# A hybrid encoder layer on one core: GLA between half-depth projection units, out-projection in two halves inside the attention stages, six places for experts

## What is computed

```python
z = rms_norm(x) @ w_in                      # 1024 -> 3088, cut into aq ak av gq gk gv ga gr
# group A, 4 heads: k and q normed; two softmax maps; chunk mask in the prompt, a cache of 512 keys per stream
p = softmax(q1 k1) - lam * softmax(q2 k2);  ao = rms_norm(p @ v) * (1 - lam_init)
# group B, 4 heads, GLA in chunks of 64 (prompt) or 16 (streams, with a state)
la = log_sigmoid(ga @ w_a2 + b_a) / 16;  b = cumsum(la)
o = (q k^T decayed by b) v + (q * exp(b)) S;  S = exp(b_last) * S + (k * exp(b_last - b))^T v
go = rms_norm(o) * silu(gr)
x = x + concat(ao, go) @ w_out
# top-1 of 4 groups, then top-2 of its 8 experts; 32 SwiGLU experts of width 256
x = x + sum_e combine_e * (silu(h @ w_gate[e]) * (h @ w_up[e])) @ w_down[e],  h = rms_norm(x)
```

## Time and profile before

| | |
|---|---|
| median of three runs | 748.46 us (747.38 to 749.25) |
| span of the profiled execution | 745.4 us; the runs lie 2.0 to 3.9 us above this span |
| granted TensorE clock, mean | 0.888 |
| busy: PE, PEld, DVE, ACT, POOL | 598.8, 395.4, 264.3, 186.4, 58.9 us |
| moved by DMA | 163.54 MB, 219 GB/s in the mean |
| chain that ended last | PE 60%, DMA 22%, DVE 8%, ACT 4%, issue 3% |

### The profile page before, as it was taken

How to read it: one execution, slowest core, us unless ns; L and a number is a source line. 1 busy time by engine, 2 the same in 40 slices (tenths; PEclk the granted TensorE clock), 3 DMA queues, 4 the chain that set the end, 5 groups by cost and what they waited for, 6 DMA issues and landing times.

```text
span 745.4 us, 8671 instructions
## 1 busy us (share of the span) xinstructions
PE 598.8 (80%) x3380; PEld 395.4 (53%) x3380; DVE 264.3 (35%) x542; ACT 186.4 (25%) x394; POOL 58.9 (8%) x93
## 2 busy tenths in 40 slices
PE   2699999999978978779799953998868687866940
PEld 2587888888865865548688843333223132322310
DVE  4811131336569447756753253110101010000006
ACT  4521233213271146556621020011010111101010
POOL 4000000000220010000000011021010102101010
PEclk9799999999996768879999955999989899989885
DMA  7011122131230176048651094499999999999639
GB/s 276 0 57 57 57 94 75 57 113 56 81 117 2 64 306 258 1 172 323 242 198 57 29 404 170 146 395 431 424 427 424 424 427 420 424 406 406 288 110 360
DMA packets 23507, 163.54 MB, mean 219 GB/s; under 512 B 4737, under 2 KB 5138, under 8 KB 10290
## 3 DMA queue, kind: packets, MB, share of 16 engines
q1 hardware_dynamic: 16290, 143.56, 48.1%
q0 software_dynamic: 6464, 16.92, 5.9%
q10 hardware_dynamic: 720, 2.62, 0.9%
HBM read 152.47 MB, written 17.43 MB: 228 GB/s over the span
## 4 chain that ended last, share of the span: by engine, by line
PE 60%; DMA 22%; DVE 8%; ACT 4%; issue 3%; POOL 1%; SPq 1%; ACTq 0%; POOLq 0%; DVEq 0%
DMA Zpad<-in_w_gu 19%; PE bank L1838 11%; PE bank L1448 7%; PE bank L1449 7%; PE bank L1450 7%; PE bank L1755 3%; PE bank L1757 3%; PE bank L1756 2%; DMA Zpad<-ye_dram 2%; PE bank L1860 2%; DVE mx L1150 1%; PE bank L1592 1%; PE bank L1776 1%; PE bank L1681 1%; PE bank L1603 1%
## 5 line engine op out<-in xcount | busy, mean ns | idle before, releaser
L1838 PE MATMUL bank<-Zpad,W 128*64 128x512 f32 x256 | 127.0, 654 | 13.6 <-DMA G<-in_w_gu 11.1
L1448 PE MATMUL bank<-W_r,hbuf_r 128*128 128x512 f32 x240 | 94.4, 393 | 3.4 <-issue 3.4
L1449 PE MATMUL bank<-W_r,hbuf_r 128*128 128x512 f32 x240 | 93.9, 391 | 0.0
L1450 PE MATMUL bank<-W_r,G_r 128*128 128x512 f32 x240 | 93.8, 391 | 0.0
L1838 PE MATMUL bank<-R,W 128*64 128x512 f32 x112 | 60.2, 699 | 30.4 <-DMA Zpad<-in_w_gu 29.5
L1394 DVE TENSOR_TENSOR W<-W,bank 128x256 f32<-128x256 f32 x16 | 6.8, 422 | 196.2 <-ACT W L886 196.2
L957 DVE TENSOR_TENSOR W_r<-W,W_r 128x2048 fp32r<-128x2048 f32 x12 | 27.5, 2291 | 104.7 <-ACT W_r L667 104.7
L1838 PEld LDWEIGHTS bank<-Zpad,W 128*64 128x64 f32 x256 | 37.1, 150 | 48.7 <-issue 45.8
L1860 PE MATMUL bank<-Zpad,W 128*64 128x512 f32 x128 | 57.9, 595 | 3.8 <-ACT W L890 3.8
L1838 PE MATMUL bank<-G,W 128*64 128x512 f32 x128 | 59.9, 623 | 0.0
L1838 PEld LDWEIGHTS bank<-R,W 128*64 128x64 f32 x112 | 17.3, 161 | 71.7 <-issue 71.7
(11 more groups left out here) (305 smaller groups left out, 983.8 us busy)
## 6 DMA issues: line engine op xcount, KB each, us to landing
Zpad<-in_w_gu SPq DMA_DIRECT2D x16, 2048.0 KB, 20.1
Zpad<-in_w_dn SPq DMA_DIRECT2D x16, 1024.0 KB, 25.8
G<-in_w_gu SPq DMA_DIRECT2D x8, 2048.0 KB, 24.2
R<-in_w_gu SPq DMA_DIRECT2D x7, 2048.0 KB, 19.0
W<-in_w_main SPq DMA_DIRECT2D x12, 1024.0 KB, 5.1
G<-in_w_dn SPq DMA_DIRECT2D x9, 1024.0 KB, 25.9
R<-in_w_dn SPq DMA_DIRECT2D x7, 1024.0 KB, 24.4
W<-in_cache_kt SPq DMA_DIRECT2D x4, 1024.0 KB, 5.6
```

The costliest lines, as they stand in the source:

```text
L1448: pe.matmul(bank[i][:, :], hH[:, d, i, :], wH[k][:, cols], start=(d == 0), stop=False)
L1449: pe.matmul(bank[i][:, :], hH[:, d, i, :], wL[k][:, cols], start=False, stop=False)
L1450: ins = pe.matmul(bank[i][:, :], hL[:, d, i, :], wH[k][:, cols], start=False, stop=(d == DC - 1))
L1838: ins = pe.matmul(bank[2 + q][CAP * j:CAP * j + CAP, :], xsT[q][:, c, j * CAP:(j + 1) * CAP], wgu[j][:, c, :], start=(c == 0), stop=(c == ...
```

## The change

It rewrites the memory plan as one arena of 49 K words per partition, and with it:

- x is transposed as loaded; norm1's gain goes into the weight halves and the token's scale into the evacuation. Weight halves are made in four slices.
- `proj(c, k, i)` is a unit of 12 matmuls. From chunk 2 on, 40 units are counted by `u`, and the pieces of GLA and the transposes of keys and queries stand between them at the units of the `U_` tables. Squares for the key and query norms, the key norm itself and the scaling of the attention outputs are GpSimd's.
- The out-projection has a GLA half (`g_step`, one step per round of the prompt attention from round 4) and an attention half (`a_step`, from round 4 of the stream attention; steps 7 to 14 behind it). A step is four transposes of a tile or twelve matmuls for half of its columns; both use one bank, 7, for tiles 0 and 1, and the sums are added to x twice.
- Keys and values of streams have three places, experts six, which are used in turn, pair by pair. The expert loops are written out.

```diff
+U_CUM, U_GT = 4, 6
+U_KT = (8, 10, 12)
+U_SC = (13, 15, 18, 20, 23)
+U_OUT = (15, 18, 20, 23, 29)
+U_SU = (25, 26, 27, 28)
+U_KTR, U_QTR = 31, 35
...
+        NKV = 3
+        EPLACE = [28 * KW, 34 * KW, 40 * KW, 5 * KW, 11 * KW, 17 * KW]
...
-            for b in range(NKV, NB):
-                sp.wait_ge(d_s_done, b - NKV + 1)
-                sp.dma_start(Kc[b % NKV], cache_kt[b]).then_inc(ld_k[b % NKV], 16)
-            for b in range(NKV, NB):
-                sp.wait_ge(d_pv_done, b - NKV + 1)
-                sp.dma_start(Vc[b % NKV], cache_v[b]).then_inc(ld_v[b % NKV], 16)
-            for n, c in enumerate(WO_ORDER):
-                sp.wait_ge(d_s_done if n < 2 else d_pv_done, NKV + n % 2 + 1)
-                sp.dma_start(wo[:, c:c + 2, :], w_out[:, c:c + 2, :]).then_inc(ld_x[n], 16)
-            sp.dma_start(egu[1], gu_rows(1)).then_inc(ld_gu[1], 16)
-            sp.dma_start(edn[1], dn_rows(1)).then_inc(ld_dn[1], 16)
-            sp.wait_ge(mT_done, 2 * NT)
-            sp.wait_ge(st_kv, 2 * NT * 16)
-            for e in (2, 0, 3):
-                if e == 0:
-                    sp.wait_ge(out_done, 2 * NT)
-                sp.dma_start(egu[e], gu_rows(e)).then_inc(ld_gu[e], 16)
-                sp.dma_start(edn[e], dn_rows(e)).then_inc(ld_dn[e], 16)
-            sp.dma_start(gu4, gu_rows(4)).then_inc(ld_gu[0], 16)
-            experts(0, 1, k0=1)
-            with sp.Fori(2, NE // 4) as g:
-                experts(0, g)
...
+                if c == 3:
+                    sp.wait_ge(b_done, 1)
+                    sp.dma_start(S0, state).then_inc(ld_state, 16)
+            sp.wait_ge(proj_done, NT * 6)
+            wo_half(H, 0)
+            wo_half(H, 1)
+            for i in range(NT):
+                sp.dma_start(X[:, i, :], x[i]).then_inc(ld_x[i], 16)
+            sp.wait_ge(st_states, 2 * 16)
+            for b in range(NKV):
+                sp.dma_start(Kc[b], cache_kt[b]).then_inc(ld_k[b], 16)
+                sp.dma_start(Vc[b], cache_v[b]).then_inc(ld_v[b], 16)
+            sp.wait_ge(out_done, 2 * NT)
+            wo_half(0, 0)
+            wo_half(0, 1)
+            for b in range(NKV, NB):
+                sp.wait_ge(d_s_done, b - NKV + 1)
+                sp.dma_start(Kc[b % NKV], cache_kt[b]).then_inc(ld_k[b % NKV], 16)
+                sp.wait_ge(d_pv_done, b - NKV + 1)
+                sp.dma_start(Vc[b % NKV], cache_v[b]).then_inc(ld_v[b % NKV], 16)
+            sp.wait_ge(d_s_done, NB)
+            sp.wait_ge(d_pv_done, NB)
+            sp.wait_ge(st_v, NT * 16)
+            for e in range(3):
+                gate_up_of(e)
+                down_of(e)
+            sp.wait_ge(out_done, 4 * NT)
+            for e in (3, 4):
+                gate_up_of(e)
+                down_of(e)
+            sp.wait_ge(tab_done, 1)
+            sp.wait_ge(idx_ready, 1)
+            gate_up_of(5)
+            down_of(5)
+            for e in range(NBUF, NE, 2):
+                sp.wait_ge(gu_done, e // 2 - 2)
+                gate_up_of(e)
+                gate_up_of(e + 1)
+                sp.wait_ge(dn_done, e // 2 - 2)
+                down_of(e)
+                down_of(e + 1)
...
+            def squares(c, kq):
+                for i in range(NT):
+                    pool.wait_ge(z_free, NT * c + i + 1)
+                    if kq:
+                        pool.wait_ge(kqred, i + 1)
+                    pool.tensor_tensor(z(C_V, i), z(c, i), z(c, i), ALU.mult).then_inc(kq_sq, 1)
+            squares(C_K, 0)
+            pool.wait_ge(rkq_ready, 1)
+            for i in range(NT):
+                kv = z(C_K, i).rearrange("p (g d) -> p g d", g=8)
+                step(pool.tensor_tensor(kv, kv, rkq[:, 0, i, :].unsqueeze(2).broadcast_to([P, 8, DH]), ALU.mult))
+                pool.tensor_tensor(kv, kv, kg[:, :].unsqueeze(1).broadcast_to([P, 8, DH]), ALU.mult
+                                   ).then_inc(k_ready, 1)
+                pool.wait_ge(k_ready, i + 1)
+                pool.dma_start(k_out[i], z(C_K, i)).then_inc(st_k, 16)
+            squares(C_Q, 1)
...
+            def w_low(c, k):
+                for s in range(4):
+                    o = slice(s * 512, (s + 1) * 512)
+                    dve.wait_ge(wH_ready, 8 * c + 4 * k + s + 1)
+                    dve.scalar_tensor_tensor(out=wL[k][:, o], in0=win[k][:, o], scalar=g1[:, 4 * k + s:4 * k + s + 1],
+                                             in1=wH[k][:, o].bitcast(F32), op0=ALU.mult, op1=ALU.subtract
+                                             ).then_inc(wL_ready, 1)
...
+            for m in range(NI + 3):
+                if m < NI:
+                    maxes(m)
+                if 5 <= m < 5 + NS:
+                    g_step(m - 5)
+                if 1 <= m <= NI:
+                    combine(m - 1)
+                if m in (1, 2):
+                    wo_low(0, m - 1)
+                if m >= 3 and (m - 3) % H == H - 1:
+                    ao_out((m - 3) // H)
...
+            def proj(c, k, i):
+                if c == 0:
+                    pe.wait_ge(hL_ready, 2 * i + k + 1)
+                elif k == 0:
+                    pe.wait_ge(z_free, NT * (c - 1) + i + 1)
+                for s in range(DC // 2):
+                    if i == 0:
+                        pe.wait_ge(wL_ready, 8 * c + 4 * k + s + 1)
+                    cs = slice(s * 512, (s + 1) * 512)
+                    d = k * DC // 2 + s
+                    pe.matmul(bank[i][:, :], hH[:, d, i, :], wH[k][:, cs], start=(d == 0), stop=False)
+                    pe.matmul(bank[i][:, :], hH[:, d, i, :], wL[k][:, cs], start=False, stop=False)
+                    ins = pe.matmul(bank[i][:, :], hL[:, d, i, :], wH[k][:, cs], start=False, stop=(d == DC - 1))
+                if k == 1:
+                    ins.then_inc(proj_done, 1)
+                elif i == NT - 1:
+                    ins.then_inc(half_done, 1)
...
+            pe.wait_ge(id_ready, 1)
+            for i in range(3):
+                x_tr(i)
+            proj(0, 0, 0)
+            x_tr(3)
+            proj(0, 0, 1)
+            x_tr(4)
+            for i in range(2, NT):
+                proj(0, 0, i)
+            for i in range(NT):
+                proj(0, 1, i)
...
+                        u = 10 * (c - 2) + 5 * k + i
+                        if u == U_CUM:
+                            cumulate()
+                        if U_GT <= u < U_GT + NT:
+                            g_tr(u - U_GT)
+                        if u in U_KT:
+                            ktok_tr(U_KT.index(u))
+                        if u in U_SC:
+                            scores(U_SC.index(u))
+                            if u != U_SC[NP]:
+                                updates(U_SC.index(u))
+                        if u in U_OUT:
+                            outputs(U_OUT.index(u))
+                        if u in U_SU:
+                            s_updates(U_SU.index(u))
+                        if U_KTR <= u < U_KTR + NT:
+                            kT_tr(u - U_KTR)
+                        if u >= U_QTR:
+                            qT_tr(u - U_QTR)
+                        proj(c, k, i)
...
+            def project_out(out, i, hf, c0, done):
+                cs = slice(hf * 512, (hf + 1) * 512)
+                for c in range(H):
+                    k, o = c // 2, (c % 2) * D + hf * 512
+                    w_high, w_low = wH[k][:, o:o + 512], wL[k][:, o:o + 512]
+                    pe.matmul(out, xH[i % 2][:, c, :], w_high, start=(c == 0), stop=False)
+                    pe.matmul(out, xH[i % 2][:, c, :], w_low, start=False, stop=False)
+                    ins = pe.matmul(out, xL[i % 2][:, c, :], w_high, start=False, stop=(c == H - 1))
+                ins.then_inc(done, 1)
+            def g_step(s):
+                i = s // 3
+                if s % 3 == 0:
+                    pe.wait_ge(mix_ready, i + 1)
+                    if i:
+                        pe.wait_ge(x2_ready, 2 * i)
+                    for h in range(H):
+                        ins = pe.transpose(bank[7][:, h * P:(h + 1) * P], z(C_GR, i, h * P, (h + 1) * P), ident[:, :])
+                    ins.then_inc(mT_done, 1)
+                    return
+                hf = s % 3 - 1
+                if hf == 0:
+                    pe.wait_ge(mL_ready, i + 1)
+                    pe.wait_ge(woL_ready, 2)
+                else:
+                    pe.wait_ge(x2_ready, 2 * i + 1)
+                project_out(bank[7][:, :], i, hf, H, out_done)
+            for m in range(NI + 3):
+                if m < NI:
+                    att_scores(m)
+                if 2 <= m < NI + 2:
+                    att_pt(m - 2)
+                if m >= 3:
+                    att_pv(m - 3)
+                if m >= 4:
+                    g_step(m - 4)
...
+                project_out(bank[7 if i < 2 or hf == 0 else 4][:, :], i, hf, 0, out_done)
+            for b in range(NB + 3):
+                if b < NB:
+                    d_scores(b)
```

(26 more changed lines are left out.)

1661 lines of the change are left out of this document (874 added, 787 removed).

## The result

The changed kernel takes **779.5 us** (median of 4 runs, 778.75 to 781.11), the kernel before, on the same chip, 748.0: ratio 1.0419, 95% interval 1.0402 to 1.0435. It is 4.2% slower. The forecast was 746.5, 722 to 770. The profiled span is 777.2 us, 31.8 more than before.

A forecast was written before the change was run, and what follows sets the result against it. Projections were taken as TensorE-bound, the middle as chains of small steps, experts as weight-bound. Terms -15.8 - 12.6 + 30.8 + 45.3 - 40.3 - 9.4 = -2.0 gave span 743.4, time 746.5 us; range 722 to 770, the forecast's own 736 to 757.

The forecast's parts named there:

- The start: Up to chunk 0's end: x transposed as it lands, first projection at 11.4 instead of 28.8; -15.8 us, bounds -18 and -8.
- GLA between the units: Before the first attention score: a 63.75 us stretch becomes 43 of work plus 8 of waits; -12.6 us, bounds -20.6 and 0.
- over the whole of these bounds it costs nothing: Key norms and squares on GpSimd: fifteen products fit in 41 us of cover if each takes under 2.5 us; 0 us.
- Prompt attention: Out-projection's GLA half merged into it: 87.0 us instead of 56.25, as rounds wait for VectorE; +30.8 us, bounds +19 and +38.
- 17.3 us for items 0 to 4: Opening prompt attention rounds, before item 5: two output weight halves on ScalarE and VectorE in a row of waits.
- Stream attention: With three places, streams 4 to 7 each wait 7.2 us for keys, bursts 5.2 us; +45.3 us, bounds +32 and +65.
- Rest of the output projection: Behind stream attention, with the router: six half-projections and two transposes left, 43.5 us instead of 83.80; -40.3 us, bounds -44 and -32.
- Place 5 with the gather: Expert weights: the sixth place is filled along with the first gather, so experts 0 to 5 are held before pair 1.
- Experts: Weight stream 223 us instead of 228.5, then 10.5 instead of 14.4 with one down projection fewer; -9.4 us, bounds -14 and 0.
- Rival 2: Stream attention: key loads take longer, 10.0 us a landing, with bursts wholly at half clock; 766.5 us, chance 0.16.
- rival 1: GLA and prompt attention: VectorE is not in the way, its adds and halves come in time; 726.5 us, chance 0.28.
- rival 3: Key norms and squares: GpSimd becomes the bound at 4 us a product, deciding from 2.5 us; 768.5 us, chance 0.08.

The follow-up runs named there:

- run 10: Kernel with all edits together (721.76 us), with VectorE's scaling of the stream states moved from unit 16 to unit 22: 719.55 us.
- run 5: Changed kernel (779.5 us), with the second half of the last chunk's weights split two units later on ScalarE and VectorE: 775.74 us.
- run 3: Changed kernel (779.5 us), with GpSimd's memsets and five scalings of the GLA output moved to around the first value store: 772.91 us.
- run 9: Changed kernel (779.5 us), with GpSimd waiting for the end of each GLA output scaling before starting the next: 774.79 us.
- run 2: Changed kernel (779.5 us), with VectorE's out-projection step put ahead of the new item's maxima in the prompt attention: 768.57 us.
- run 1: Changed kernel (779.5 us), with SyncE's queue reordered in the stream attention, keys of streams 3 to 6 asked for ahead of stream 3's values: 747.27 us.
- run 4: Changed kernel (779.5 us), with expert 5's 3 MB asked for when the first gather has landed instead of with it: 771.61 us.
- run 6: Changed kernel (779.5 us), with the GLA half of the output projection behind the prompt attention instead of inside it, using three banks: 783.4 us.

## Why the prediction was wrong

The direction of each costed term was right, the sum was not: 33.8 us too low on the span, and the forecast's own range (to 757) and the full one (to 770) were both too narrow.

- **The start** (-15.8; measured -13.2). The first projection came at 14.80, not 11.4: TensorE's queue has the transposes of tiles 1 and 2 ahead of it, and these tiles lie behind the cols and the first 1 MB of weights in SyncE's queue. They started at 11.47 and took 3.67 us. I had moved the weights on the path and forgotten the tiles.
- **GLA between the units** (-12.6; -6.65). The 63.75 us became 57.1 (63.75 - 6.65). TensorE idles 11.1 us between chunk 1 and the first score (168.28 less 157.19) where I took 8, and the work beside it is 46 us where I took 43. "The units around it keep the clock full" is the step that failed there: behind the clearest wait, the one before tile 1's output, the granted clock is 0.50 from 149.59 to 153.87. That wait is 4.46 us instead of 3, in part since VectorE's two scalings took 3.31 us beside GpSimd's square instead of 2 x 1.22 (run 10 prices it at 2.2); the waits around the query norms are 2.05 us (run 5).
- **GpSimd's products.** The step "over the whole of these bounds it costs nothing" was right on the price, 1.04 to 1.28 us a product; the estimate of 1.12 us from the Trainium skill (GPSIMD Engine Reference, 3.1 Elementwise) agrees. It failed in what was not asked: whether GpSimd's work costs *VectorE* anything. The five scalings of the GLA output, which I did not cost at all, held VectorE for 6 us at the start of the attention (runs 3 and 9). The Trainium skill has a mechanism (SBUF — State Buffer, Who interferes with whom): a scaling of VectorE in a two-port mode needs a port pair that GpSimd uses too; whoever issues first has the pair for the whole instruction, and the other is fully blocked. The rows agree that it is held (6.03 us for 0.17), but over two memsets and five products and not over one instruction; no view shows in which mode it ran.
- **Prompt attention** (+30.8; +41.0, above my bound of +38). The step that failed is "17.3 us for items 0 to 4": it took 21.9, for the 6 us above (16.8 in run 3, without them). The rounds were right one by one (6.44 and 4.15 us for 6.4 and 4.2; 6.0 for 5.9 at 384 keys), but two took more. The first half-projection's, 7.6 us for 5.4 (269.15 to 276.70), ran at a granted clock of 0.59, which I had not priced. The one of 8.9 us for 5.9 (301.10 to 309.95) has the output of a finished tile on ScalarE and VectorE ahead of the half-projection's operand: TensorE waits 2.07 us for it, and goes on at half clock for three more. The reason that I gave for the rounds of 6.4 us, VectorE's step behind the maxima, is shown by run 2.
- **Stream attention** (+45.3; +50.8). The mechanism, the queue's order and the clock behind each wait were right (run 1). Mis-sized were two terms of the sum, by 2.7 and 2.6 us. The burst of 5.2 us took 5.9 to 6.3 in three of five cases (366.16 to 372.02, 392.61 to 398.89), at a granted clock of 0.56 to 0.60; the first and the last took 5.3 and 5.2. Of the four waits of 7.2 us from the end of a burst to the next scores, three took 7.2 to 7.3, but the last 9.7 (398.89 to 408.58), its load 9.26; why that load was slower stays open. I put that price on "having three places"; it belongs to the order in which they are filled again.
- **Rest of the output projection** (-40.3; -40.2) and routing: right, the former with some luck: 27.0 us to the last projection for 25.8, and 16.6 behind it for 17.7.
- **The gather.** "Place 5 with the gather" was read as a gain of a place, with no cost. The gather is on the path and shares the DMA engines with what was asked for just ahead of it: +5.8, of which run 4 takes back 5.6.
- **Experts** (-9.4; -5.7), within its bounds. The stream is shorter as forecast: from the end of the first gate and up to the start of the last it takes 221.5 us (511.90 to 733.45) for 227.0 (474.40 to 701.41). The step that failed is "one down projection less" behind the last weights. In both kernels two down projections follow (at 740.53 and 745.42; before at 708.50 and 713.65), so this part takes 15.6 us for 15.9 where I had taken 3.9 off.

Rival 2 (key loads longer, 766.5) was the nearest in time, but its condition, waits of 9.5 us, held for one stream of four; rival 1 (VectorE not in the way) is refuted by run 2, rival 3 by the 1.04 us product. None joined several terms, and the terms slipped together: most were waits put at their shortest chain, with the half clock behind them left out or priced too low. A range for such a sum has to allow for the upper sides of several terms at once; GLA, prompt attention and stream attention alone at their upper bounds would have given 746.5 + 12.6 + 7.2 + 19.7 = 786. The two signs of being wrong, a stream stage under 60 us and a first score later than 250, did not come (81.7 and 247.25): both looked at single terms and not at the sum.

## What to carry to other kernels

- Work laid inside another stage can gain little more than TensorE idles there, and often less: the stream stage idled 0.5 us and grew by 17.2 for 11.8 us of work (run 1), the prompt stage idled 24.6 of 66.8 us (run 6) and hid 6 of 36 us as built and 17 with VectorE's order mended. Ask first which engine releases TensorE in the merged round, and put that engine's old step ahead of the new round's.
- When places become few, look at the queue that refills them: a load that the next instruction needs must not stand behind one that waits for a later release. That alone was 32 us of 779.
- A load that nobody needs yet, issued just ahead of a small one on the path, costs the small one its time (9.33 us for 4.56), and a helper engine's cost is also what it does to its neighbour.

## What the runs showed of the hardware

- VectorE's scaling of 128x2 elements, 0.17 us by itself, was held for 6.03 us by two memsets and five products that followed each other on GpSimd without a gap, and for 2.05 and 1.05 us when GpSimd waited for the end of each product. It was let in at a gap, not at the next product's start. A VectorE product of 128x1 elements, 0.15 us by itself, was held only to the end of the GpSimd product then running (0.49 us, run 9's section), though another followed without a gap.
- GpSimd's product of two 128x512 tensors took 1.04 us, 1.28 where the second was one row of 64 repeated.
- Behind idle stretches of TensorE of 4.3 to 7.2 us the scores of a stream took 1.93 to 1.94 us for 1.04, and the bursts that they begin had a granted clock of 0.56 to 0.69; with a single wait for keys, of 2.6 us, the stage's clock stayed at 0.96 and the same 585 matmuls took 9 us less.
- A gather of 128 rows took 9.33 us when 3 MB had been asked for 0.5 to 0.9 us ahead of it, and 4.56 us when they were asked for behind it.
